# Attention weights of the second sample divided by their sums on two engines instead of one

## The chip, the cores and the metric

The kernel runs on one core of a Trainium2 chip. A core has TensorE (matrix products, called PE in the profile), VectorE (DVE), ScalarE (ACT), GpSimd (POOL) and SyncE (SP), which issues most transfers. The metric is the device time of one execution in microseconds.

## The reference, cut to what matters

The model is one inference step of a four-layer network on 128 context tokens (the first sample, s = 0) and 128 latent tokens (the second, s = 1). Layers 0 and 3 mix tokens by an mLSTM, layer 1 by windowed attention with a learned sink, layer 2 by neighbourhood attention; each layer ends in a convolutional FFN. The change touches the attention of layers 1 and 2 alone:

```python
def _attend(q, parts, sink):
    scale = q.shape[-1] ** -0.5
    logits = []
    for k_, v_, bias in parts:
        s = jnp.einsum('bkgqd,bksd->bkgqs', q, k_).astype(jnp.float32) * scale
        if bias is not None:
            s = s + bias
        logits.append(s)
    ...
    p = jax.nn.softmax(jnp.concatenate(logits, axis=-1), axis=-1)
    out, off = None, 0
    for k_, v_, _ in parts:
        n = k_.shape[2]
        o = jnp.einsum('bkgqs,bksd->bkgqd', p[..., off:off + n].astype(v_.dtype), v_)
        out = o if out is None else out + o
        off += n
    return out
```

A context token reads the 128 context keys; a latent token reads 128 latent keys and 128 keys of a cache, so its weights are twice as wide. Each of 16 heads has its own softmax, whose last step divides the exponentials by their sum.

## The kernel before, in words

Every engine has an instruction list written out by hand; semaphores join them. Weights stream from memory as 1 MB tiles through four buffers `raw`; ScalarE rounds each half tile to `spl_hi` (L488), VectorE takes the remainder `spl_lo` (L499, 128x1024 values, both inputs in SBUF, the on-chip memory), and TensorE multiplies both parts. A buffer is loaded again once its tile is split or used. Between other work TensorE runs `fill`, which multiplies tiles of another stream, the modulation weights (L755).

Attention works in eight units of four heads. Unit u belongs to head group u // 2 and to sample u % 2, so odd units are those of the second sample, with weights of 256 columns a head instead of 128. A unit passes through:

- `scores` on TensorE (L1027), into the banks SCORES, of which there is one pair: the next unit's scores wait for the exponentials of this one.
- `maxima` on VectorE: the largest score of each head (L2217, in layer 2 for odd units L2223 to L2227), and its negative `nm` (L2230 in layer 1, L2236 in layer 2), a 128x4 instruction. L2230 reads `mx` and `nsink`, L2236 reads `mx`, all in SBUF.
- `exps` on ScalarE (L1566): exponentials into `Ea[u % 2]`, and their sums.
- `reciprocals` on VectorE (L2248): `rsum`, one number a head, and in layer 1 before it L2244.
- the division, on GpSimd (L2525): `Ea` times `rsum`, in place, one instruction for the four heads, with the semaphore `pn_done` at its end.
- `weights` on TensorE (L1043): transposes of `Ea`, after `pn_done`; copied out by ScalarE and, for odd units, VectorE (L2252).
- `values` on TensorE (L1063), copied out by ScalarE as `O_hi`, with the remainder `O_lo` from VectorE in `attended` (L2257).

The units overlap: VectorE's list in layer 1 reads, from unit 3 on, `maxima(u)`, `reciprocals(u)`, `weights(u - 1)` when u - 1 is odd, `attended(u - 2)`, `maxima(u + 1)`. In layer 2 the projections of the queries, keys and values (`half_rows`, L692) lie between the units of the first half, and VectorE's list holds their splits (L499) and the copies of their results to `qrow`, `krow` and `vrow` (L2200). TensorE waits for such a copy (semaphore `row_d`) before it starts the projection that reuses the bank, at L1155 and L1165.

Of the kernel before, what the change touches and what calls it, by code (L numbers as in the profile page):

```python
# [19 lines left out]
ALU = mybir.AluOpType  # L20
# [3 lines left out]
P = 128  # L24
# [4 lines left out]
TOK = NS * T  # L29
# [284 lines left out]
def build(nc, io):  # L314
# [128 lines left out]
    def v3(ap, b):  # L443
        return ap.rearrange("p (a b) -> p a b", b=b)
# [4 lines left out]
    def beside(t, g, e):  # L449
# [13 lines left out]
        z_silu z_mul z_hi z_lo  # L463
        up_hi up_sum tg_done cg_half cg_done tv_done cv_half cv_done sg_done gt_done ghi_done glo_done
        cache_landed bias_landed row_a row_d row_k row_v roped tq_mm tq_a tq_d tk_mm tk_a tk_d kv_landed
        s_mm nm_done exp_done esink_in esink_done rsum_done pn_done pt_mm pt_a pt_d o_mm o_hi o_lo
        xa_done yt_mm yrow_a yrow_d y_landed""".split()
    S = {n: nc.alloc_semaphore(n) for n in names}
    raw_landed = [S[f"raw{r}"] for r in range(RAW)]
# [83 lines left out]
    with nc.Block() as block:  # L553
# [41 lines left out]
        def _(pe):  # L595
# [387 lines left out]
            def attention(i):  # L983
# [48 lines left out]
                def weights(u):  # L1032
                    s = u % 2
                    w = 8 * a + u
                    pe.wait_ge(S["pn_done"], w + 1)
                    if w:
                        pe.wait_ge(S["pt_a"], w)
                    if w // 2:
                        pe.wait_ge(S["pt_d"], w // 2)
                    for b in range(1 + s):  # L1040
                        for p in range(4):
                            o = (4 * b + p) * T
                            mm = pe.transpose(ACC[2 + b][:, p * T:(p + 1) * T], Ea[s][:, o:o + T], ident)  # L1043
                    mm.then_inc(S["pt_mm"], 1)
# [720 lines left out]
        def _(dve):  # L1765
# [424 lines left out]
            def attention(i):  # L2190
# [48 lines left out]
                def reciprocals(u):  # L2239
                    w = 8 * a + u  # L2240
                    dve.wait_ge(S["exp_done"], 4 * w + 4)
                    if a == 0:
                        dve.wait_ge(S["esink_done"], w + 1)
                        link(dve.tensor_tensor(sums[:, :], sums[:, :], esink[:, :], ALU.add))  # L2244
                        link.wait()
                    if w:
                        dve.wait_ge(S["pn_done"], w)
                    dve.reciprocal(rsum[:, :], sums[:, :]).then_inc(S["rsum_done"], 1)  # L2248

                def weights(u):  # L2250
                    dve.wait_ge(S["pt_mm"], 8 * a + u + 1)
# [204 lines left out]
        @block.gpsimd  # L2456
        def _(pool):
            chain = Link(pool, "pool_chain")
            zeroed = [gI, gF, gA, gM, gb, gc, gG, gz]
            for t in zeroed:  # L2460
                pool.memset(t[:, :], 0.0).then_inc(S["misc_init"], 1)
            pool.memset(half_pow[:, :], -0.5).then_inc(S["misc_init"], 1)
            assert len(zeroed) + 1 == MISC_INIT

            pool.memset(credit[0:1, 6:7], 0.0).then_inc(S["xcs_done"], 2)
            pool.wait_ge(S["misc_init"], MISC_INIT)
            pool.wait_ge(S["loads"], 16)

            def square_total(q):

                done = 3 * q
                for k in range(3):
                    pool.wait_ge(S["sq_done"], 5 * q + (2, 3, 3)[k])
                    if k:
                        pool.wait_ge(S["sqa_done"], done + k)
                    elif q:
                        pool.wait_ge(S["ssq_mm"], q)
                    out, a, b = ((sqa[:, :], sq[0][:, :], sq[1][:, :]), (sqa[:, :], sqa[:, :], sq[0][:, :]),
                                 (sqa[:, 0:TOK], sqa[:, 0:TOK], sqa[:, TOK:2 * TOK]))[k]
                    pool.tensor_tensor(out, a, b, ALU.add).then_inc(S["sqa_done"], 1)  # L2480

            def norm(q):
                square_total(q)
                pool.wait_ge(S["xvar_done"], q + 1)
                pool.tensor_tensor(rstd[:, :], var[:, :], half_pow[:, :], ALU.pow).then_inc(S["rstd_done"], 1)

            for i in range(DEPTH):
                norm(2 * i)
                if MIXER[i] == "mlstm":
                    j = ML_INDEX[i]  # L2490
                    for t in range(8):
                        pool.wait_ge(S["xc_done"], 8 * j + t + 1)
                        o = COL["ml_skip"] + j * KI + 2 * t
                        skip = small[:, o:o + 2]
                        pool.tensor_tensor(v3(XCS[:, t * 512:(t + 1) * 512], TOK), v3(ow[t % 2][:, :], TOK),
                                           skip.unsqueeze(2).to_broadcast([P, 2, TOK]),
                                           ALU.mult).then_inc(S["xcs_done"], 1)
                    for h in range(MH):
                        q = 4 * j + h
                        weights = v3(ST[:, h * TOK:(h + 1) * TOK], TOK)  # L2500
                        pool.wait_ge(S["e_done"], 5 * q + 5)
                        if h >= 2:
                            pool.wait_ge(S["den_mm"], q - 1)
                        pool.tensor_tensor(v3(Pw[h % 2][:, :], TOK), v3(E[h % 2][:, :], TOK),
                                           weights.to_broadcast([P, 2, TOK]), ALU.mult).then_inc(S["p_done"], 1)
                        pool.wait_ge(S["den_done"], q + 1)
                        pool.wait_ge(S["den_mm"], q + 1)
                        chain(pool.tensor_tensor(Pw[h % 2][:, :], Pw[h % 2][:, :], den[h % 2][:, :], ALU.mult))
                        chain.wait()
                        pool.tensor_tensor(PT[:, h * TOK:(h + 1) * TOK], Pw[h % 2][:, 0:TOK], Pw[h % 2][:, TOK:2 * TOK],  # L2510
                                           ALU.add).then_inc(S["pt_done"], 1)
                    for h in range(MH):
                        q = 4 * j + h
                        pool.wait_ge(S["var_done"], q + 1)
                        if q:
                            pool.wait_ge(S["hn_done"], 2 * q)
                        chain(pool.tensor_scalar(var[:, :], v3(mv[:, :], 2)[:, :, 1], 1.0, EPS, ALU.mult, ALU.add))
                        chain.wait()
                        pool.tensor_tensor(rstd[:, :], var[:, :], half_pow[:, :], ALU.pow).then_inc(S["root_done"], 1)
                else:  # L2520
                    for u in range(8):
                        width = (1 + u % 2) * T
                        pool.wait_ge(S["rsum_done"], 8 * (i - 1) + u + 1)
                        ev = v3(Ea[u % 2][:, 0:4 * width], width)
                        pool.tensor_tensor(ev, ev, rsum[:, :].unsqueeze(2).to_broadcast([P, 4, width]),  # L2525
                                           ALU.mult).then_inc(S["pn_done"], 1)
                norm(2 * i + 1)

            norm(2 * DEPTH)
# [22 lines left out]
```

## Time and profile before

| What | Value |
|---|---|
| Time, median of 3 runs | 1843.75 us (1842.93 to 1846.68) |
| The profiled execution's own time | 1840.74 us |
| Its span, first to last instruction | 1839.1 us |
| TensorE busy | 1793.7 us, 98% |
| VectorE busy | 1389.5 us, 76% |
| ScalarE busy | 1002.4 us, 55% |
| GpSimd busy | 143.8 us, 8% |
| HBM traffic | 228 GB/s over the span |
| The granted clock of TensorE, mean | 0.996 |

The attention units of layer 1 lie between 655 and 705 us of the span, those of layer 2 between 960 and 1041 us. A share of busy time is a mean over stages; in both stretches the other engines hand work to and fro in short steps, and who waits for whom is read from the timeline.

### The profile page before, as it was taken

The page shows a single profiled execution, that of the slowest core. Times are in us where ns is not written, and L with a number is a line of the kernel's source. Part 1 is how long each engine was busy: PE and PEld are TensorE (multiplying, and loading weights), DVE is VectorE, ACT ScalarE, POOL GpSimd, SP SyncE. Part 2 cuts the span into 40 slices and gives each one's busy share as a digit, 9 for nine tenths or more (in the row PEclk, how much of TensorE's full clock was granted, in tenths as well). Part 3 has the DMA queues.
Part 4 walks back from the last instruction along what each step waited for, and adds up shares of the span by engine and source line. Part 5 has one row for each costly group of instructions (what it writes and reads, how often), then busy time and mean ns, then how long its engine had stood idle before and what let it go on. Part 6 is the DMA issues. An engine that isn't in the chain of part 4 may idle for free.

```text
span 1839.1 us, 27506 instructions
## 1 busy us (share of the span) xinstructions
PE 1793.7 (98%) x11032; PEld 1494.3 (81%) x11032; DVE 1389.5 (76%) x2140; ACT 1002.4 (55%) x1567; POOL 143.8 (8%) x122
## 2 busy tenths in 40 slices
PE   5999999999999999999999999999999999999998
PEld 3988877797888867888977778888888787878888
DVE  3854777668898767999865698988665877779984
ACT  3744445446674454776354466745653445456753
POOL 1100121000000011000101100001100210010001
PEclk8999999999999999999999999999999999999999
DMA  9565656857665766675674777566555746445552
GB/s 393 211 225 197 203 207 242 307 221 292 261 216 205 288 250 265 252 277 198 216 311 166 298 283 294 204 224 266 207 185 183 240 163 225 171 172 195 197 173 80
DMA packets 74318, 421.27 MB, mean 229 GB/s; under 512 B 12400, under 2 KB 18952, under 8 KB 26576
## 3 DMA queue, kind: packets, MB, share of 16 engines
q1 hardware_dynamic: 56016, 395.68, 57.5%
q10 hardware_dynamic: 18176, 23.85, 4.0%
q8 instruction: 87, 1.43, 0.3%
q14 instruction: 39, 0.32, 0.0%
HBM read 408.51 MB, written 10.96 MB: 228 GB/s over the span
## 4 chain that ended last, share of the span: by engine, by line
PE 86%; DVE 5%; issue 3%; DMA 2%; ACT 2%; POOL 1%; SPq 0%; ACTq 0%; POOLq 0%; DVEq 0%
PE ps L654 17%; PE ps L676 10%; PE ps L711 9%; PE ps L657 9%; PE ps L636 6%; PE ps L692 5%; PE ps L714 5%; PE ps L639 3%; PE ps L622 3%; PE ps L624 3%; PE ps L623 3%; PE ps L755 3%; DMA raw<-in_stream 2%; DVE spl_lo L499 2%; PE ps L962 1%
## 5 line engine op out<-in xcount | busy, mean ns | idle before, releaser
L499 DVE TENSOR_TENSOR spl_lo<-raw,spl_hi 128x1024 fp32r<-128x1024 f32 x556 | 690.0, 1266 | 148.4 <-ACT spl_hi L488 147.1
L488 ACT ACTIVATE spl_hi<-raw 128x1024 fp32r<-128x1024 f32 x556 | 574.2, 1053 | 299.9 <-PE ps L714 109.5
L654 PE MATMUL ps<-H,spl_hi 128*128 128x512 f32 x1408 | 444.4, 397 | 3.7 <-DVE H L1854 2.9
L657 PEld LDWEIGHTS ps<-H,spl_lo 128*128 128x128 f32 x1408 | 264.5, 188 | 62.5
L657 PE MATMUL ps<-H,spl_lo 128*128 128x256 f32 x1408 | 276.7, 278 | 0.0
L654 PEld LDWEIGHTS ps<-H,spl_hi 128*128 128x128 f32 x1408 | 214.3, 189 | 17.9 <-issue 14.2
L711 PE MATMUL ps<-G,spl_hi 128*128 128x512 f32 x528 | 165.8, 395 | 0.0
L636 PE MATMUL ps<-B,spl_hi 128*128 128x512 f32 x512 | 160.8, 395 | 0.0
L622 PE MATMUL ps<-H,spl_hi 128*128 128x256 f32 x512 | 148.3, 290 | 1.8 <-DVE spl_lo L499 1.1
L623 PE MATMUL ps<-H,spl_hi 128*128 128x256 f32 x512 | 145.2, 284 | 0.0
L624 PE MATMUL ps<-H,spl_lo 128*128 128x256 f32 x512 | 145.0, 283 | 0.0
L676 PE MATMUL ps<-spl_hi,A 128*128 128x512 f32 x512 | 140.0, 391 | 0.5 <-ACT v L1267 0.5
L714 PEld LDWEIGHTS ps<-G,spl_lo 128*128 128x128 f32 x528 | 99.2, 188 | 23.4
L639 PEld LDWEIGHTS ps<-B,spl_lo 128*128 128x128 f32 x512 | 96.2, 188 | 22.7
L676 PEld LDWEIGHTS ps<-spl_hi,A 128*128 128x128 f32 x512 | 95.2, 188 | 21.7 <-issue 2.3
L755 PE MATMUL ps<-raw,cond_wide 128*32 128x512 f32 x704 | 94.6, 632 | 17.3 <-DMA raw<-in_stream 17.3
L1267 ACT ACTIVATE up<-ps 128x512 f32<-128x512 f32 x88 | 52.6, 598 | 105.2 <-PE ps L657 105.1
L622 PEld LDWEIGHTS ps<-H,spl_hi 128*128 128x128 f32 x512 | 98.4, 192 | 11.5 <-issue 9.8
L714 PE MATMUL ps<-G,spl_lo 128*128 128x256 f32 x528 | 103.7, 278 | 0.0
L639 PE MATMUL ps<-B,spl_lo 128*128 128x256 f32 x512 | 100.6, 278 | 0.0
L623 PEld LDWEIGHTS ps<-H,spl_hi 128*128 128x128 f32 x512 | 98.5, 192 | 0.8 <-issue 0.7
L624 PEld LDWEIGHTS ps<-H,spl_lo 128*128 128x128 f32 x512 | 98.5, 192 | 0.0
(251 smaller groups left out, 2927.4 us busy)
## 6 DMA issues: line engine op xcount, KB each, us to landing
raw<-in_stream SPq DMA_DIRECT2D x366, 1024.0 KB, 5.0
out_new_C<-c_stage ACTq DMA_DIRECT2D x16, 512.0 KB, 3.8
column<-in_ada_cols SPq DMA_DIRECT2D x16, 512.0 KB, 5.3
cond_all<-cond_out ACTq DMA_DIRECT2D x3, 1024.0 KB, 7.3
ada_b<-in_ada_b ACTq DMA_DIRECT2D x3, 768.0 KB, 9.1
E<-rows_out ACTq DMA_DIRECT2D x8, 256.0 KB, 4.3
Em<-rows_out ACTq DMA_DIRECT2D x8, 256.0 KB, 4.5
x<-in_x SPq DMA_DIRECT2D x1, 1024.0 KB, 6.7
```

The costliest lines, as they stand in the source:

```text
L488: act.activation(spl_hi[m % SPL][:, :], raw[r % RAW][:, h * HALF:(h + 1) * HALF], ACT.Copy).then_inc(S["hi_done"], 1)
L499: dve.tensor_tensor(spl_lo[m % SPL][:, :], raw[r % RAW][:, h * HALF:(h + 1) * HALF], spl_hi[m % SPL][:, :].bitcast(F32), ALU.subtract).the ...
L622: pe.matmul(out, w_hi, x_hi, start=st, stop=False, skip_group_check=True)
L623: pe.matmul(out, w_hi, x_lo, start=False, stop=False, skip_group_check=True)
L624: mm = pe.matmul(out, w_lo, x_hi, start=False, stop=en, skip_group_check=True)
L636: pe.matmul(v3(banks[b][:, :], TOK), spl_hi[m % SPL][:, c], B_both[:, kk], start=kk == 0, stop=False, skip_group_check=True)
L639: mm = pe.matmul(banks[b][:, 0:TOK], spl_lo[m % SPL][:, c], B_both[:, kk, 0], start=False, stop=kk == KI - 1, skip_group_check=True)
L654: pe.matmul(banks[:, b * 512:(b + 1) * 512], spl_hi[m % SPL][:, c], H[:, kk * 512:(kk + 1) * 512], start=kk == 0, stop=False, skip_group_c ...
L657: mm = pe.matmul(banks[:, b * 512:b * 512 + TOK], spl_lo[m % SPL][:, c], H[:, kk * 512:kk * 512 + TOK], start=False, stop=kk == KD - 1, sk ...
L676: mm = pe.matmul(ACC[2 * s + c][:, :], a, w[m % SPL][:, c * 512:(c + 1) * 512], start=st, stop=en, skip_group_check=True)
L711: pe.matmul(v3(bank[:, :], TOK) if nk == KI else bank[:, :], spl_hi[m % SPL][:, b], rows(k), start=st, stop=False, skip_group_check=True)
L714: mm = pe.matmul(ps[2 * pair + o][:, 0:TOK], spl_lo[m % SPL][:, b], x_hi, start=False, stop=en, skip_group_check=True)
```

## The change

In an odd unit GpSimd now divides the weights of the first two heads only (128x512 values instead of 128x1024). VectorE, right after its reciprocal, divides those of the other two, with two instructions of 128x256 values, and signals a new semaphore `pn_half`; TensorE's transposes of an odd unit wait for both semaphores. Even units stay as they are. VectorE first waits for its own reciprocal (`rsum_done`), which is also what GpSimd waits for.

```diff
--- before.py
+++ after.py
@@ -463,7 +463,7 @@
         z_silu z_mul z_hi z_lo
         up_hi up_sum tg_done cg_half cg_done tv_done cv_half cv_done sg_done gt_done ghi_done glo_done
         cache_landed bias_landed row_a row_d row_k row_v roped tq_mm tq_a tq_d tk_mm tk_a tk_d kv_landed
-        s_mm nm_done exp_done esink_in esink_done rsum_done pn_done pt_mm pt_a pt_d o_mm o_hi o_lo
+        s_mm nm_done exp_done esink_in esink_done rsum_done pn_done pn_half pt_mm pt_a pt_d o_mm o_hi o_lo
         xa_done yt_mm yrow_a yrow_d y_landed""".split()
     S = {n: nc.alloc_semaphore(n) for n in names}
     raw_landed = [S[f"raw{r}"] for r in range(RAW)]
@@ -1033,6 +1033,8 @@
                     s = u % 2
                     w = 8 * a + u
                     pe.wait_ge(S["pn_done"], w + 1)
+                    if s:
+                        pe.wait_ge(S["pn_half"], w // 2 + 1)
                     if w:
                         pe.wait_ge(S["pt_a"], w)
                     if w // 2:
@@ -2246,6 +2248,12 @@
                     if w:
                         dve.wait_ge(S["pn_done"], w)
                     dve.reciprocal(rsum[:, :], sums[:, :]).then_inc(S["rsum_done"], 1)
+                    if u % 2:
+                        dve.wait_ge(S["rsum_done"], 8 * a + u + 1)
+                        for k in range(2, 4):
+                            o = slice(k * TOK, (k + 1) * TOK)
+                            ins = dve.tensor_scalar(Ea[1][:, o], Ea[1][:, o], rsum[:, k:k + 1], None, ALU.mult)
+                        ins.then_inc(S["pn_half"], 1)
 
                 def weights(u):
                     dve.wait_ge(S["pt_mm"], 8 * a + u + 1)
@@ -2521,8 +2529,9 @@
                     for u in range(8):
                         width = (1 + u % 2) * T
                         pool.wait_ge(S["rsum_done"], 8 * (i - 1) + u + 1)
-                        ev = v3(Ea[u % 2][:, 0:4 * width], width)
-                        pool.tensor_tensor(ev, ev, rsum[:, :].unsqueeze(2).to_broadcast([P, 4, width]),
+                        n = 4 - 2 * (u % 2)
+                        ev = v3(Ea[u % 2][:, 0:n * width], width)
+                        pool.tensor_tensor(ev, ev, rsum[:, 0:n].unsqueeze(2).to_broadcast([P, n, width]),
                                            ALU.mult).then_inc(S["pn_done"], 1)
                 norm(2 * i + 1)
 
```

VectorE's list around the reciprocal of unit 3 in layer 1, before. `sums`, `rsum` and `mx` are the sums, their reciprocals and the maxima; `Ea_128` in the second list is the buffer of the odd units.

```order
L2244 TENSOR_TENSOR sums<-sums,esink 128x4 [waits esink_done,exp_done]
L2248 RECIPROCAL rsum<-sums 128x4 [waits pn_done,dve_link]
L2257 TENSOR_TENSOR O_lo<-ps,O_hi 128x2x128 [waits o_hi]
L2217 TENSOR_REDUCE mx<-ps 128x2 [waits s_mm]
L2217 TENSOR_REDUCE mx<-ps 128x2
L2230 SCALAR_TENSOR_TENSOR nm<-mx,nsink 128x4 [waits dve_link]
L2233 TENSOR_TENSOR esink<-nm,nsink 128x4 [waits nm_done]
```

The same place in the changed kernel:

```order
L2246 TENSOR_TENSOR sums<-sums,esink 128x4 [waits esink_done,exp_done]
L2250 RECIPROCAL rsum<-sums 128x4 [waits pn_done,dve_link]
L2255 TENSOR_SCALAR Ea_128<-Ea_128,rsum 128x256 [waits rsum_done]
L2255 TENSOR_SCALAR Ea_128<-Ea_128,rsum 128x256
L2265 TENSOR_TENSOR O_lo<-ps,O_hi 128x2x128 [waits o_hi]
L2219 TENSOR_REDUCE mx<-ps 128x2 [waits s_mm]
L2219 TENSOR_REDUCE mx<-ps 128x2
L2232 SCALAR_TENSOR_TENSOR nm<-mx,nsink 128x4 [waits dve_link]
L2235 TENSOR_TENSOR esink<-nm,nsink 128x4 [waits nm_done]
```

Two multiplications stand between the reciprocal and the `O_lo` of unit 1, ahead of the maxima of unit 4. The same two stand behind the reciprocal of every odd unit, eight times in all.

GpSimd's list at the start of layer 1's units, before:

```order
L2525 TENSOR_TENSOR Ea_127<-Ea_127,rsum 128x512 [waits rsum_done]
L2525 TENSOR_TENSOR Ea_128<-Ea_128,rsum 128x1024 [waits rsum_done]
L2525 TENSOR_TENSOR Ea_127<-Ea_127,rsum 128x512 [waits rsum_done]
L2525 TENSOR_TENSOR Ea_128<-Ea_128,rsum 128x1024 [waits rsum_done]
L2525 TENSOR_TENSOR Ea_127<-Ea_127,rsum 128x512 [waits rsum_done]
```

And in the changed kernel:

```order
L2534 TENSOR_TENSOR Ea_127<-Ea_127,rsum 128x512 [waits rsum_done]
L2534 TENSOR_TENSOR Ea_128<-Ea_128,rsum 128x512 [waits rsum_done]
L2534 TENSOR_TENSOR Ea_127<-Ea_127,rsum 128x512 [waits rsum_done]
L2534 TENSOR_TENSOR Ea_128<-Ea_128,rsum 128x512 [waits rsum_done]
L2534 TENSOR_TENSOR Ea_127<-Ea_127,rsum 128x512 [waits rsum_done]
```

The instructions of the odd units (`Ea_128`) have half as many columns; nothing else has moved there.

## Rows read from the trace of the kernel before

**Rows 1.** Page: the span, and the chain that ended last, by engine.

```profile
span 1839.1 us, 27506 instructions
...
PE 86%; DVE 5%; issue 3%; DMA 2%; ACT 2%; POOL 1%; SPq 0%; ACTq 0%; POOLq 0%; DVEq 0%
```

**Rows 2.** Groups, GpSimd: count | busy us, mean ns | idle before.

```profile
L2525 POOL TENSOR_TENSOR Ea<-Ea,rsum 128x1024 f32<-128x1024 f32 x8 | 15.1, 1893 | 40.7 <-DVE rsum L2248 40.7
...
L2525 POOL TENSOR_TENSOR Ea<-Ea,rsum 128x512 f32<-128x512 f32 x8 | 8.3, 1040 | 123.9 <-DVE rsum L2248 123.9
```

**Rows 3.** Waits of TensorE: us in total, times, longest us.

```profile
PE ps L1043 <- POOL Ea L2525: 4.5, 5, 2.0
```

**Rows 4.** The chain in order of time, layer 1: start us, us, what.

```profile
679.01 1.50 ACT Ea L1566 x8
...
683.22 0.17 DVE nm L2230
...
685.40 0.72 PE ps L1027 x8
...
689.63 1.07 PE ps L1027 x8
```

**Rows 5.** Timeline of VectorE, layer 1: start us, us; idle before it in brackets.

```profile
667.80 0.68 DVE L1773 TENSOR_TENSOR mod_b<-ps,ada_b 128x512 f32<-128x512 f32 x1
...
669.17 0.70 DVE L2230 SCALAR_TENSOR_TENSOR nm<-mx,nsink 128x4 f32<-128x4 f32 x1
...
685.74 0.18 DVE L2248 RECIPROCAL rsum<-sums 128x4 f32<-128x4 f32 x1
...
686.24 0.42 DVE L2257 TENSOR_TENSOR O_lo<-ps,O_hi 128x256 fp32r<-128x256 f32 x1 [0.31 <-ACT O_hi L1267]
...
687.36 0.56 DVE L2230 SCALAR_TENSOR_TENSOR nm<-mx,nsink 128x4 f32<-128x4 f32 x1
```

**Rows 6.** Timeline of GpSimd, layers 1 and 2 (odd units).

```profile
667.97 1.89 POOL L2525 TENSOR_TENSOR Ea<-Ea,rsum 128x1024 f32<-128x1024 f32 x1 [3.59 <-DVE rsum L2248]
...
686.00 1.89 POOL L2525 TENSOR_TENSOR Ea<-Ea,rsum 128x1024 f32<-128x1024 f32 x1 [3.80 <-DVE rsum L2248]
...
975.83 1.89 POOL L2525 TENSOR_TENSOR Ea<-Ea,rsum 128x1024 f32<-128x1024 f32 x1 [5.77 <-DVE rsum L2248]
...
992.77 1.90 POOL L2525 TENSOR_TENSOR Ea<-Ea,rsum 128x1024 f32<-128x1024 f32 x1 [8.50 <-DVE rsum L2248]
...
1023.73 1.89 POOL L2525 TENSOR_TENSOR Ea<-Ea,rsum 128x1024 f32<-128x1024 f32 x1 [6.01 <-DVE rsum L2248]
```

**Rows 7.** Timelines of VectorE and GpSimd in a norm, 713 to 717 us.

```profile
713.23 1.22 DVE L499 TENSOR_TENSOR spl_lo<-raw,spl_hi 128x1024 fp32r<-128x1024 f32 x1
...
713.38 2.21 POOL L2480 TENSOR_TENSOR sqa<-sq,sq 128x512 f32<-128x512 f32 x1 [16.55 <-ACT sq L1284]
...
714.36 2.32 DVE L499 TENSOR_TENSOR spl_lo<-raw,spl_hi 128x1024 fp32r<-128x1024 f32 x1
```

**Rows 8.** Timeline of VectorE, layer 2.

```profile
977.00 2.94 DVE L499 TENSOR_TENSOR spl_lo<-raw,spl_hi 128x1024 fp32r<-128x1024 f32 x2 [1.25 <-ACT spl_hi L488]
...
994.21 2.67 DVE L499 TENSOR_TENSOR spl_lo<-raw,spl_hi 128x1024 fp32r<-128x1024 f32 x2 [0.53 <-ACT spl_hi L488]
...
1025.06 0.58 DVE L2236 TENSOR_SCALAR nm<-mx 128x4 f32<-128x4 f32 x1
```

**Rows 9.** Timeline of TensorE, layer 2.

```profile
980.64 0.47 PE L692 MATMUL ps<-spl_hi,H 128*128 128x512 f32 x1 [1.18 <-issue]
...
997.59 0.47 PE L692 MATMUL ps<-spl_hi,H 128*128 128x512 f32 x1 [0.19 <-issue]
...
1027.29 1.14 PE L1027 MATMUL ps<-kT,qT 64*128 64x256 f32 x8
```

**Rows 10.** Groups by line and form, VectorE.

```profile
L1991 DVE TENSOR_SCALAR gM<-gF 36x256 f32<-36x256 f32 x2 | 0.6, 277 | 0.0
...
L2452 DVE TENSOR_SCALAR yrow<-ps,rstd 128x256 f32<-128x256 f32 x4 | 1.7, 478 | 0.8 <-POOL rstd L2485 0.8
```


## The prediction

> **What bounds the kernel now.** The profile's page comes first: TensorE is busy for nearly the whole span and 86% of the chain that ended last is its own [rows 1]. So a microsecond that TensorE waits in attention is a microsecond of the time, unless it would have waited later anyway. Next, the list of TensorE's waits: it waited for GpSimd's division 5 times, 4.5 us in all [rows 3]. That is all that a faster division can hand to TensorE directly. The groups by form give the price of a division: 1893 ns for an odd unit, 1040 ns for an even one [rows 2], so that half the columns save 0.85 us.
>
> The chain then tells the two layers apart. In layer 1 from 655 us to 685.40 it runs between VectorE and ScalarE: maxima, `nm`, exponentials (1.50 us for an even unit), sums, reciprocal, and on to the next maxima [rows 4]. From 685.40 on it is TensorE's. In layer 2 it is mostly TensorE's, with short waits in it [rows 9].
>
> Last, the timelines show something that the groups hide. `nm` of unit 5 took 0.17 us [rows 4]; `nm` of unit 6 took 0.56, and that of unit 2 took 0.70 [rows 5]. Both ended when GpSimd's division did, at 686.00 + 1.89 = 687.89 and 667.97 + 1.89 = 669.86 [rows 6]. So VectorE is held up while GpSimd works. It is the same in layer 2: a pair of splits took 2.94 and 2.67 us, and the 0.58 us `nm` of unit 6 ended at 1025.64, when the division begun at 1023.73 was over [rows 6, 8]. The norm shows the other direction. Splits began at 713.23, GpSimd's addition at 713.38, the second split at 714.36. The first split took its normal 1.22 us. The addition ended at 715.59, that is 1.14 us after the first split; the second split took 2.32 us and ended 1.09 us after the addition [rows 7]. The engines took turns, and the waiting GpSimd went ahead of VectorE's next instruction. The first split's end at 714.45 also shows that an instruction that isn't held starts 0.09 us before the end of the one ahead.
>
> **The change, part by part.** Let r be the end of an odd unit's reciprocal. GpSimd starts at r + 0.08 (685.92 against 686.00) and before was done at r + 1.97 [rows 5, 6].
>
> *Price of one multiplication on VectorE.* No row shows 128x256 from SBUF to SBUF with one number a partition. The nearest are 277 ns (36x256, SBUF to SBUF) and, above, 478 ns (128x256 out of PSUM, with such a number) [rows 10]. I take 0.30 us, since the first has the same memories and columns.
>
> *What the two engines do together.* Both wait for `rsum_done`. VectorE follows itself in some 0.04 us (an estimate: `nm` of unit 5 began at 683.22 and ended at 683.39, and the next step shown in the chain waits no longer than that on it), GpSimd in 0.08. By the turns of [rows 7]: first multiplication until r + 0.34; then GpSimd, whose addition kept 1.14 us after its grant where I take 0.90 for the shorter division (1.04 less the same start of about 0.14 that ran while it was held), until r + 1.24; then the second multiplication, 0.19 us more, until **r + 1.43**. TensorE's weights are ready 0.54 us sooner than before, but VectorE goes on 1.43 us later. What stands behind it is, in turn, `mod_b` and the maxima, `O_lo` and the maxima, a split, or the maxima alone.
>
> *Layer 1, unit 1.* r = 667.89. `mod_b` began at 667.80 [rows 5]; now at 669.32 - 0.09 = 669.23, 1.43 later. `nm` (begun at 669.17) is then free at 670.60 and no longer held, and done at 670.77; before it was done at 669.87. Chain +0.90.
> *Unit 5.* r = 685.92, VectorE free at 687.35. `O_lo` began at 686.24 after 0.31 us idle; now at 687.26, +1.02. `nm` would end at 687.36 + 1.02 + 0.17 = 688.55 against 687.92: +0.63. Unit 3 is built in the same way (its `nm` too took 0.56 us) and costs +0.63.
> The exponentials of unit 6 are thus 2.16 us late. TensorE needs them for its scores at 689.63; they ended at about 687.95 + 1.50 = 689.45, so 0.18 us are slack [rows 4]. **Layer 1: +2.0.** Unit 7 adds nothing: no maxima follow it and the transposes behind are long covered by the output projection.
>
> *Layer 2, unit 1.* r = 975.75. VectorE is free at 977.18, the splits begin at 977.09 instead of 977.00 but are not held: they end at 977.09 + 2.35 = 979.44 against 979.94. The copy `qrow` behind them is what TensorE waited for, 1.18 us before 980.64 [rows 8, 9]: **-0.5**.
> *Unit 3.* r = 992.69, free at 994.12; `O_lo` and then the splits, from about 994.38, end at 996.73 against 996.88: **-0.15**, out of the 0.19 us that TensorE waited at 997.59.
> *Unit 5.* r = 1023.65, free at 1025.08. The maxima of unit 6 took 0.79 us up to `nm` at 1025.06, so began at 1024.27; now at 1024.99. `nm` ends at 1025.95 against 1025.64, +0.3. TensorE's next scores, at 1027.29 [rows 9], came 0.15 us after the exponentials ended (1025.64 + 1.50): **+0.2**. Unit 7's splits wait for a tile from memory: nothing.
> Layer 2: -0.45.
>
> **The sum** is 2.0 - 0.45 = **+1.6 us**. The profiled execution took 1840.74 us and would take 1842.3. That execution lies 3.0 us below the median of the runs, to which I add the same 1.6: **1845.3 us**. VectorE's eight pairs, 8 x 0.6 = 5 us of work, would be nothing to an engine that is 76% busy; they cost only where they lie in the chain.
>
> **A rule against the trace.** Whether the multiplication holds GpSimd out at all, no row shows: [rows 7] are instructions with two inputs in SBUF, and the `nm` of [rows 8], with one input, was the one that was held. The Trainium skill ("SBUF — State Buffer", section "Who interferes with whom") states that VectorE's `tensor_scalar`, when input and output are in SBUF, may run in a mode that takes the ports shared with GpSimd, and that whichever starts first keeps them for the whole instruction. By that rule the turns above hold; were the multiplication to use VectorE's own ports alone, it would be the first rival. That page of the Trainium skill advises to let the engine off the critical path wait, and here it is VectorE, on the path, that does.
>
> **The rivals.**
> *No turns: VectorE does both, or they don't hinder each other.* VectorE is free at r + 0.55, GpSimd done at r + 1.45 at the latest. In layer 1 `nm` of units 2, 4 and 6 comes at 0.0, -0.24 and -0.24, of which TensorE can use 0.2. In layer 2 unit 1 gives -0.45, unit 3 -0.19, unit 5 -0.5 (`nm` not held after 1025.1, and TensorE's transposes as much earlier), unit 7 -0.1. In sum -1.4: 1842.3. For it: the second multiplication is queued 0.2 us after the first, before a late GpSimd may have asked; against: GpSimd's addition, asked for 0.15 us after the split's start, went first.
> *Slower: the turns, at high prices.* If a multiplication takes 0.48 us (the upper row), GpSimd keeps the ports for its full 1.04 us and the second multiplication costs 0.33 after it, VectorE is free at r + 1.89, 0.46 later. That adds to three units of layer 1 and four places of layer 2: 7 x 0.46 = +3.2, in all +4.8: 1848.6. It decides from 0.3 us more, r + 1.73, on. For it: [rows 7] show grants of full length for VectorE; against: short instructions there lose only what they wait for.
> *Faster by more than measurable: the waits go.* If TensorE's 4.5 us for GpSimd vanished with nothing in their place, -4: 1839.8. Against it: only odd units change, and the chain between VectorE and ScalarE is no shorter.
>
> **How the numbers follow.** A change below 0.2% (3.7 us) can't be told from none by this measurement. My forecast, +1.6 with turns: 60%. No turns, -1.4: 23%. Both are within 0.2%, less a few per cent for runs that lie apart by as much as the three above (1842.93 to 1846.68). Slower with high prices: 13%. Faster: 4%. So faster 0.05, same 0.80, slower 0.15. The range reaches from the second case, less 1.3 for the runs' own spread, to the edge of the third: 1841.0 to 1849.0; the likeliest alone would be 1843.5 to 1847.5.
>
> **What would show it.** In the trace after: the multiplications (L2255) as a short one of 0.3 us and one of about 1.2 that ends after GpSimd; GpSimd's odd divisions about 1.15 us long instead of 1.89; `nm` in layer 1 at 0.17 us throughout; the exponentials of unit 6 about 2 us later, counted from those of unit 0; TensorE's wait at the first projection behind unit 1 in layer 2 down from 1.18 to 0.7 us. I am wrong if both multiplications are short (first rival), or if GpSimd goes first, which costs as much as the turns. I would be wrong in size if a later wait, say for a tile of weights, swallows the 2 us of layer 1; between 705 and 960 us I found no wait of TensorE that large.

## The result, and the profile after

The changed kernel took **1849.56 us** (median of 7 runs, 1847.53 to 1852.26) against 1843.75 (1842.93 to 1846.68). The ratio is 1.0031, with an interval of 1.002 to 1.0043: slower by 5.8 us, beyond the 1849.0 at which the predicted range ends. The profiled execution took 1850.99 us.

Two later sets of runs put the same pair at 1.0015 (1.0006 to 1.0024, +3.1 us) and 1.0014 (1.0005 to 1.0024, +2.3 us). All three intervals lie above 1, so the sign is firm; the size lies between 2 and 6 us. In the later sets the kernel before had medians of 1844.9 to 1845.2 us, some 1.3 above the first set's, and the changed kernel 1848.06 and 1847.48, 1.5 and 2.1 below its first. Why the sets differ by so much is open.

The page of the changed kernel: its span, and the chain that ended last, by engine, as in [rows 1].

```profile
span 1849.0 us, 27529 instructions
...
PE 87%; DVE 5%; issue 3%; DMA 2%; ACT 2%; POOL 1%; SPq 0%; ACTq 0%; POOLq 0%; DVEq 0%
```

The span is 9.9 us longer and the chain's shares are the same to a point: it is still TensorE's. Not all of the 9.9 us are the change's: layer 1's first `nm` begins at 660.12 us where it began at 657.83, so 2.3 us lie ahead of anything that was changed.

The sum was made in attention, so layer 1 comes first. VectorE behind the reciprocal of unit 1 (start us, us, then engine, line, operation; idle time before it in brackets). Lines L2217, L2230, L2244 and L2248 of before are now L2219, L2232, L2246 and L2250; the multiplications are L2255.

```profile
670.00 0.18 DVE L2250 RECIPROCAL rsum<-sums 128x4 f32<-128x4 f32 x1
670.21 1.50 DVE L2255 TENSOR_SCALAR Ea<-Ea,rsum 128x256 f32<-128x256 f32 x2
671.63 0.68 DVE L1775 TENSOR_TENSOR mod_b<-ps,ada_b 128x512 f32<-128x512 f32 x1
672.23 0.74 DVE L2219 TENSOR_REDUCE mx<-ps 128x2 f32<-128x256 f32 x2
673.00 0.16 DVE L2232 SCALAR_TENSOR_TENSOR nm<-mx,nsink 128x4 f32<-128x4 f32 x1
```

The pair of multiplications takes 1.50 us. `nm` is back at 0.16 us, as forecast (0.70 in [rows 5]). The two multiplications apart, from two narrow windows, are one of 1.23 us:

```profile
670.21 1.23 DVE L2255 TENSOR_SCALAR Ea<-Ea,rsum 128x256 f32<-128x256 f32 x1
```

and one of 0.34:

```profile
671.37 0.34 DVE L2255 TENSOR_SCALAR Ea<-Ea,rsum 128x256 f32<-128x256 f32 x1
```

GpSimd at the same place:

```profile
670.26 1.04 POOL L2534 TENSOR_TENSOR Ea<-Ea,rsum 128x512 f32<-128x512 f32 x1 [3.59 <-DVE rsum L2250]
...
682.37 1.04 POOL L2534 TENSOR_TENSOR Ea<-Ea,rsum 128x512 f32<-128x512 f32 x1 [5.97 <-DVE rsum L2250]
```

GpSimd's division takes 1.04 us, no more than an even unit's [rows 2], though it begins 0.05 us behind VectorE's in the records. So the turn went to **GpSimd first**: the first multiplication was held until GpSimd's division was over at 671.30 and ended 0.14 us later; the second ran free, in 0.34 us. All eight pairs look like this: over the 16 multiplications the durations are 339 ns at least and 1233 at most. The Trainium skill ("SBUF — State Buffer", section "Who interferes with whom") says that `tensor_scalar` within SBUF can take the ports shared with GpSimd, and that whichever of the two issues first keeps them. The trace agrees that a multiplication is held; by the recorded starts, with VectorE 0.05 us ahead, the one that began second went first here, so for the order the measurement decides. No run shows which of the multiplication's reads or writes is held.

VectorE is free at r + 1.53 (r = 670.18), where the forecast had r + 1.43. Then TensorE:

```profile
669.57 0.72 PE L1027 MATMUL ps<-kT,qT 64*128 64x128 f32 x8 [0.99 <-ACT Ea L1568]
672.36 1.11 PE L771 MATMUL ps<-small,mod_b 128*128 128x128 f32 x4 [2.07 <-DVE mod_b L1775]
673.27 1.91 PE L1045 MATMUL ps<-small,Ea 128*128 128x128 f32 x8
675.11 1.12 PE L1065 MATMUL ps<-PTa,vrow 128*64 128x128 f32 x8
676.16 2.04 PE L1027 MATMUL ps<-kT,qT 64*128 64x256 f32 x8
678.13 1.09 PE L1002 MATMUL ps<-small,qrow 128*128 128x128 f32 x8
```

The same instructions in the kernel before:

```profile
667.28 0.72 PE L1027 MATMUL ps<-kT,qT 64*128 64x128 f32 x8 [0.98 <-ACT Ea L1566]
668.53 0.66 PE L771 MATMUL ps<-small,mod_b 128*128 128x128 f32 x4 [0.54 <-DVE mod_b L1773]
669.91 1.09 PE L1043 MATMUL ps<-small,Ea 128*128 128x128 f32 x8 [0.72 <-POOL Ea L2525]
670.93 0.66 PE L1063 MATMUL ps<-PTa,vrow 128*64 128x128 f32 x8
671.52 1.14 PE L1027 MATMUL ps<-kT,qT 64*128 64x256 f32 x8
```

Two things differ. First, L771 waited 0.54 us for `mod_b` before and now waits 2.07. This is a wait that the forecast never priced: it saw `mod_b` late in VectorE's list and asked only what that does to the maxima behind it. Second, from then until 678 every group of matmuls takes 1.7 to 1.8 times as long: 1.91 for 1.09 (eight transposes), 1.12 for 0.66, 2.04 for 1.14. The windows of that stretch say why (columns: busy us and count of TensorE, of its weight loads, of VectorE, ScalarE, GpSimd; then the granted clock, the DMA share, GB/s):

```profile
668.00:672.00 4.00, 1.30 (x16) 0.53 (x8) 3.90 (x10) 2.10 (x10) 1.04 (x1) 0.90 0.96 334
672.00:676.00 4.00, 3.64 (x20) 3.14 (x20) 2.36 (x10) 2.20 (x10) 0.64 (x1) 0.50 0.81 336
676.00:678.00 2.00, 2.00 (x12) 1.21 (x8) 0.50 (x2) 0.38 (x1) 0.40 (x1) 0.50 0.00 0
1070.00:1080.00 10.00, 10.00 (x59) 5.11 (x59) 7.00 (x22) 6.01 (x18) 0.70 (x1) 0.83 0.98 410
```

In the kernel before (1062 to 1072 is the same piece of work as 1070 to 1080 above):

```profile
668.00:672.00 4.00, 2.75 (x24) 2.16 (x26) 2.36 (x8) 2.09 (x11) 1.86 (x1) 1.00 1.02 422
672.00:676.00 4.00, 4.00 (x44) 2.55 (x40) 3.18 (x9) 2.38 (x9) 1.04 (x1) 1.00 0.05 18
1062.00:1072.00 10.00, 9.54 (x64) 5.24 (x64) 7.56 (x23) 6.49 (x18) 0.70 (x1) 1.00 0.95 398
```

From 672 to 678 us the granted clock is 0.50, the 1.2 GHz level instead of 2.4. A mean of 0.90 from 668 to 672 puts the fall 0.8 us before 672, when TensorE had waited 0.99 us for exponentials and was in the wait of 2.07; the low clock lasts 6.8 us. It falls for 3.4 us in each of the norms behind the two layers as well (a mean of 0.58 from 732 to 736 us, and the last window above); in this profile of the kernel before it was 1.00 there.

In layer 2 what the forecast read from VectorE's list came as it said: the splits behind unit 1 take 2.35 us for 2.94, and `nm` of unit 6 takes 0.17 for 0.58 [rows 8]:

```profile
984.30 2.35 DVE L499 TENSOR_TENSOR spl_lo<-raw,spl_hi 128x1024 fp32r<-128x1024 f32 x2
986.58 0.68 DVE L2202 COPY qrow<-ps 128x512 f32<-128x512 f32 x1
...
1032.52 0.17 DVE L2238 TENSOR_SCALAR nm<-mx 128x4 f32<-128x4 f32 x1
```

In the list of TensorE's waits (us in total, times, longest) GpSimd's division of [rows 3] is gone; what the division touches is now:

```profile
PE ps L1027 <- ACT Ea L1568: 4.8, 7, 1.0
PE ps L771 <- DVE mod_b L1775: 4.0, 3, 2.1
...
PE ps L1045 <- DVE Ea L2255: 1.6, 1, 1.6
```

The same list of the kernel before:

```profile
PE ps L771 <- DVE mod_b L1773: 2.5, 3, 1.2
PE ps L1027 <- ACT Ea L1566: 2.2, 4, 1.0
```

The 4.5 us for GpSimd came back as 2.6 more for exponentials, 1.5 more for `mod_b` and 1.6 for VectorE's own division (in the last unit of layer 2, where before GpSimd was waited for 2.0).

To compare many kernels, one measure serves below: the time from the start of the first `nm` of a layer to the start of the last `O_lo` of its units, what lies between, and what lies behind, read from the starts in each profile (us). "Half clock" is how long the granted clock was 0.50 in layer 1's units.

| Profile | Layer 1 | between | Layer 2 | behind | half clock |
|---|---|---|---|---|---|
| before, three profiles | 44.51, 44.53, 44.54 | 261.22, 261.28, 260.29 | 76.94, 77.14, 76.97 | 798.60, 799.43, 799.35 | 0, 0, 0 |
| changed, three profiles | 49.32, 49.37, 47.29 | 261.22, 261.24, 260.16 | 77.62, 76.76, 76.77 | 800.72, 800.15, 800.44 | 6.8, 6.8, 0 |

The second and third profile of each are the controls of the next section. The mean difference is +4.1 in layer 1, 0.0 in layer 2 (two of three profiles have -0.2, the first lost 0.7 more, most of it in the last unit, where ScalarE waited 0.99 us for a tile from memory), +1.3 behind: +5.4 us. What lies ahead of layer 1 scatters by more than 2 us in both kernels (its first `nm` begins at 657.83, 659.32 and 660.35 us before, at 660.12, 659.98 and 658.14 in the changed one).

### The profile page after: what moved, and what is told of

It is laid out like the page before. It is cut to its first block, busy times and chain, and to the rows that moved or that the text cites. A ratio compares the mean times of both kernels' runs of the same rounds, so it can differ in the third digit from the quotient of the medians.

```text
span 1849.0 us, 27529 instructions
## 1 busy us (share of the span) xinstructions
PE 1800.1 (97%) x11032; PEld 1499.0 (81%) x11032; DVE 1398.2 (76%) x2156; ACT 1002.4 (54%) x1567; POOL 137.1 (7%) x122
## 3 DMA queue, kind: packets, MB, share of 16 engines
q8 instruction: 87, 1.43, 0.3%
## 4 chain that ended last, share of the span: by engine, by line
PE 87%; DVE 5%; issue 3%; DMA 2%; ACT 2%; POOL 1%; SPq 0%; ACTq 0%; POOLq 0%; DVEq 0%
PE ps L654 18%; PE ps L676 9%; PE ps L711 9%; PE ps L657 9%; PE ps L636 6%; PE ps L692 5%; PE ps L714 5%; PE ps L639 3%; PE ps L755 3%; PE ps L622 3%; PE ps L624 3%; PE ps L623 3%; DMA raw<-in_stream 2%; DVE spl_lo L499 1%; PE ps L962 1%
```

## The experiments

My theory was that the added cost is VectorE held by GpSimd (the ports), which makes TensorE wait in layer 1 behind unit 1 and brings the clock down. The rivals: the multiplications are simply too much work for VectorE; or something between or behind the layers, and not the attention, takes the time.

**One unit alone, and all the others.** A table chooses which odd units are divided on both engines; the second kernel has `SPLIT = (3, 5, 7, 9, 11, 13, 15)`.

```diff
+SPLIT = (1,)
...
-                    if s:
-                        pe.wait_ge(S["pn_half"], w // 2 + 1)
+                    if w in SPLIT:
+                        pe.wait_ge(S["pn_half"], SPLIT.index(w) + 1)
...
-                    if u % 2:
+                    if w in SPLIT:
...
-                        n = 4 - 2 * (u % 2)
+                        n = 2 if 8 * (i - 1) + u in SPLIT else 4
```

> Only unit 1 of layer 1 is divided on two engines, the other seven odd units as in the kernel before. Theory A (VectorE is held until 1.5 us after its reciprocal, which lengthens the chain, and in this unit TensorE's 2.1 us wait for mod_b lets the granted clock fall to 1.2 GHz for some 6 us): +1.0 us of chain and +2.0 us of clock, +3 us over the kernel before, and a stretch at clock 0.5 after that unit. Theory B (the chain alone costs, the low clock is hidden behind it): +1 us. Theory C (the cost is spread over the span and not in these units): +0.7 us, an eighth of the whole.

> The seven other odd units are divided on two engines, unit 1 of layer 1 as before. Theory A: no stretch at the low clock, the whole change less 3 us: +2.5 to +3 us over the kernel before. Theory B: +4.8 us. Theory C: +5 us.

Unit 1 alone: 1.001 (1.0001 to 1.0019), layer 1 at 47.81 us with 6.8 us at half the clock. The others: 1.0001 (0.9993 to 1.001), layer 1 at 46.21 at full clock. Over before these are +3.30 and +1.70, together +5.0, where both at once gave +4.8: in layer 1 the parts add up. Of unit 1's 3.3, some 2.0 come with the half clock; at full clock its share is +1.0 (worked out in the next section), less than the +1.7 of the others. By the times the two kernels are slower than before by 1.8 and 0.4 us (medians 1846.81 and 1845.41 against 1845.02), where theory A had +3 and +2.5 to +3: both sizes were missed, and only their sum, +2.2, fits the two later sets of the changed kernel.

**`mod_b` ahead of the multiplications.** The same two multiplications, but TensorE's wait at L771 is taken away.

```diff
-                    reciprocals(1)
-                    copy_mod(i, 1)
+                    reciprocals(1, lambda: copy_mod(i, 1))
```

(`reciprocals` calls it between the reciprocal and the multiplications.)

> The changed kernel with the copy mod_b of layer 1 moved ahead of the two multiplications of unit 1, so that TensorE's transposes of it wait 1.5 us less; the maxima of unit 2 come as late as in the changed kernel. Theory A: TensorE's wait for mod_b is back near 0.5 us, the clock stays at full, 2 us less than the changed kernel: +3.5 to +4 us over the kernel before. Theory B: as the changed kernel, +5.8 us.

Layer 1 took 46.69 us at full clock; the wait at L771 was 0.53 again. The time was 1.0013 (1.0004 to 1.0022), +2.1 us, which is what layer 1's +2.2 says, and less than the +3.5 to +4 expected: without the long wait the chain between VectorE and ScalarE is still late. It is 0.6 us less late than in the changed kernel at full clock (47.29, below), because `mod_b` now runs while GpSimd holds the multiplications: the copy and the pair together take as long as the pair alone did, and `nm` comes 0.6 us sooner.

**TensorE kept busy in the gap.** Eight matmuls of no use stand ahead of L771.

```diff
+                    pe.wait_ge(S["row_a"], 2)
+                    pe.wait_ge(S["row_d"], 2)
+                    for _ in range(8):
+                        pe.matmul(ACC[0][:, :], H[:, 0:P], H[:, 0:512], start=True, stop=True, skip_group_check=True)
```

> The changed kernel with eight matmuls of 512 columns, whose result nothing reads, placed on TensorE between the scores of unit 2 and the transposes of mod_b in layer 1; they fill 1.7 of the 2.1 us that it waits there. Nothing comes earlier. Theory A: the clock stays at full, 2 us less than the changed kernel, +3.5 to +4 us over the kernel before. Theory B: as the changed kernel, +5.8 us.

Layer 1 took 47.28 us at full clock and the whole 1.0019 (1.001 to 1.0028), +3.0 us. At first I read this as proof that the idle time brings the clock down. It is not: the third profile of the changed kernel, without the added matmuls, has the same 47.29 at full clock with the wait of 2.07 in place:

```profile
670.38 0.66 PE L771 MATMUL ps<-small,mod_b 128*128 128x128 f32 x4 [2.07 <-DVE mod_b L1775]
670.87 1.04 PE L1045 MATMUL ps<-small,Ea 128*128 128x128 f32 x8
671.84 0.66 PE L1065 MATMUL ps<-PTa,vrow 128*64 128x128 f32 x8
672.78 1.14 PE L1027 MATMUL ps<-kT,qT 64*128 64x256 f32 x8 [0.28 <-ACT Ea L1568]
```

So the long wait is followed by the half clock in some executions and not in others, and neither the fill nor `mod_b` ahead shows anything on that. The same rows show that the wait of 2.07 us costs nothing by itself: layer 1 is as long with it as with the matmuls in its place.

**Controls.** The kernel before and the changed one, run again in two sets.

> The kernel before once more, beside the three others. All theories: no difference from itself; its ratio shows what this measurement tells from nothing. By stages of its trace, the span from the first nm of layer 1 to the last O_lo of its units took 44.5 us, and should again.

> The changed kernel once more, on the chip of the others. Its units of layer 1 took 49.3 us, 4.8 us more than before, those of layer 2 0.7 more. If the whole of the loss lies there, it is slower by 4 to 6 us again; with the low clock at the same place in the trace.

> The kernel before, a third profile: does the clock stay at full in layer 1's units? In two of its profiles it did, but it fell there in the kernel that changes layer 2 alone, whose layer 1 is the same code. If its steps stay 44.5 us at full clock here too, the low clock is rare without the change; if not, it is chance in every kernel and the share of the change in it is smaller than 2 us.

> The changed kernel, a third profile. If its 2.1 us wait for mod_b brings the low clock every time, layer 1 takes 49.3 us again; if it is chance, 47.3 us with the clock at full. Time: 3 to 6 us over the kernel before, as in the two measurements so far (5.8 and 3.1 us).

Before: 0.9999 (0.9991 to 1.0008) and 0.9994 (0.9985 to 1.0004). Changed: 1.0015 (1.0006 to 1.0024) and 1.0014 (1.0005 to 1.0024). Their stages are in the table above. What repeats to 0.1 us is layer 1 at a given clock; what scatters by about 1 us is the stretch between and the stretch behind, and by over 2 us the stretch ahead.

The mean granted clock of every run is known as well, and it limits what the table shows. The three profiles of the kernel before ran at 0.996, 0.997 and 0.997, while the 152 runs of that kernel in the four later sets have a mean of 0.9944 (0.989 to 0.998): the usual execution has more half clock than these three show. The changed kernel's 30 runs have a mean of 0.9938, none above 0.996. The difference of 0.0006 has the right sign, but the runs of one kernel scatter by 0.002, so it is hardly clear of chance.

**All four heads on VectorE in odd units, GpSimd out.** Twice the multiplications, but nothing beside them.

```diff
-                        for k in range(2, 4):
+                        for k in range(4):
...
-                        ins.then_inc(S["pn_half"], 1)
+                        ins.then_inc(S["pn_done"], 1)
...
+                        if u % 2:
+                            continue
```

> In odd units VectorE divides all four heads, GpSimd none. If the two engines hinder each other as the trace of the changed kernel shows (first multiplication 1.23 us, second 0.34), then twice the multiplications without GpSimd beside them are done sooner: four of 0.34 us, VectorE free 1.1 us after the reciprocal instead of 1.5. Layer 1: 1.2 us less than the changed kernel, and 2 us less again if TensorE's wait for mod_b, then 1.7 us, no longer lowers the clock. Rival, that each multiplication is slow by itself or that the work counts and not the ports: VectorE free after 2 us or more, slower than the changed kernel.

```profile
667.99 0.18 DVE L2248 RECIPROCAL rsum<-sums 128x4 f32<-128x4 f32 x1
668.20 1.14 DVE L2253 TENSOR_SCALAR Ea<-Ea,rsum 128x256 f32<-128x256 f32 x4
```

Four multiplications on their own take 1.14 us, less than two beside GpSimd (1.50); each takes 0.35. The kernel is at 0.9998 (0.9989 to 1.0006), layer 1 at 46.57 us with 3.4 us at half the clock, layer 2 at 75.93. Too much work for VectorE is thereby out as the main cause: doubling it makes the kernel no slower than before. It isn't free in layer 1: each of the pairs of steps around units 3 and 5, at full clock, takes 9.32 us, 0.38 more than before (0.7 to 1.1 more with GpSimd beside). Layer 2 gains 1.1.

**Two heads divided, by VectorE alone.** Heads 0 and 1 of odd units are left undivided, so this kernel leaves out a part of the softmax; GpSimd idles there.

```diff
-                        ins.then_inc(S["pn_half"], 1)
+                        ins.then_inc(S["pn_done"], 1)
...
+                        if u % 2:
+                            continue
```

> Work is left out: in odd units VectorE divides heads 2 and 3 and nobody divides heads 0 and 1, so GpSimd is idle there. The order of all else is that of the changed kernel. It prices the two multiplications without GpSimd beside them. If the ports are what costs: 0.6 us for the two instead of 1.50, TensorE's wait for mod_b 1.2 us instead of 2.1, and the units of layer 1 take 44.5 to 45.2 us instead of 49.3, as in the kernel before. If the instructions themselves cost: 47 us or more.

```profile
670.32 0.62 DVE L2253 TENSOR_SCALAR Ea<-Ea,rsum 128x256 f32<-128x256 f32 x2
670.85 0.69 DVE L1773 TENSOR_TENSOR mod_b<-ps,ada_b 128x512 f32<-128x512 f32 x1
```

0.62 us for the pair, layer 1 at 44.82 us, within 0.3 of before, at full clock; L771 waits 1.19 us; the time is 0.9995 (0.9986 to 1.0003). The same VectorE instructions with GpSimd beside them took 47.29 at full clock. **The 2.5 us between are what GpSimd's simultaneous work costs**, one profile against one, and the whole agrees: 0.9995 without it, 1.0014 and 1.0015 with it. GpSimd's own part isn't what is waited for, since it is over 0.4 us before VectorE's pair. That it costs through shared ports is the reading of the held and unheld durations.

**The multiplications behind the maxima.** In four units VectorE divides after the next `nm`, when GpSimd is done.

```diff
-                    if u % 2:
-                        dve.wait_ge(S["rsum_done"], 8 * a + u + 1)
...
+                def divided(u):
+                    dve.wait_ge(S["rsum_done"], 8 * a + u + 1)
...
+                    divided(1)
```

(`divided(u)` has the loop over the two heads. It stands behind `maxima(u + 1)` for units 1, 3 and 5 of layer 1 and unit 5 of layer 2; for the other four odd units it stands right behind the reciprocal, as in the changed kernel. The reciprocal also waits for `pn_half` of the unit before.)

> The division on two engines, but VectorE's two multiplications stand behind the next unit's maxima (units 1, 3, 5 of layer 1 and 5 of layer 2), where VectorE waits 1.5 us for ScalarE. My theory: GpSimd is done by then, nothing in the chain is late, nm is no longer held: layer 1 takes 43.7 to 44.5 us, layer 2 0.2 less than before; within 1 us of the kernel before or faster by 1. Rival, that a division which ends 0.2 us later than before holds TensorE back: layer 1 45 us or more.

```profile
670.17 0.66 PE L771 MATMUL ps<-small,mod_b 128*128 128x128 f32 x4 [0.54 <-DVE mod_b L1775]
671.80 1.76 PE L1045 MATMUL ps<-small,Ea 128*128 128x128 f32 x8 [0.97 <-issue]
673.49 1.12 PE L1065 MATMUL ps<-PTa,vrow 128*64 128x128 f32 x8
```

The pair took 0.61 us in the four moved places, still 1.50 in the other four, and the chain kept its 4.08 us a step in unit 1, but now TensorE's weights come late: the transposes began 0.97 us after L771 and the clock fell for 3.4 us. Layer 1 took 46.74 us where 43.7 to 44.5 was expected, the whole 1.0002 (0.9993 to 1.0011). The rival that was named came true: units 3 and 5, at full clock, cost 0.3 us each as well. The wait had moved from `mod_b` to the weights.

**Layer 2 alone.** The split there only, `SPLIT = (9, 11, 13, 15)`, run in two sets; and the odd units of layer 2 on VectorE alone, layer 1 as before.

> The division on two engines in layer 2 alone. Layer 1 as before (44.5 us); layer 2 0.2 to 0.4 us shorter than before, as in the trace of the second run of the changed kernel. If the low clock that the changed kernel's trace shows in the norm behind layer 2 belongs to this layer's units, it is here too and the stretch behind takes 1 us more; if it belongs to what layer 1 has shifted, it isn't. Time within 1.5 us of the kernel before.

> The division on two engines in layer 2 alone, again. Its trace showed 0.3 us less in layer 2 than before and nothing elsewhere, its times 3.5 us less by the medians (ratio 0.9988). If the times were right, it is faster by 2 us or more again; if the trace is, no difference can be told.

> Layer 1 as before; in layer 2 VectorE divides all four heads of odd units, GpSimd none. From the trace of the kernel in which VectorE does so in both layers: layer 1 44.5 us, layer 2 75.9 instead of 77.0, the rest as before: 1.1 us faster, less than this measurement can tell. Rival, that the gain of layer 2 is lost in the norm behind it: no difference in the span either.

The split: 0.9988 (0.9979 to 0.9996) at first, then 0.9999 (0.999 to 1.0008). The traces have layer 2 at 76.82 and 76.75 us against 77.0, so 0.2 to 0.3 us of gain; the 3.5 us of the first set have no place in the trace and did not come again. The two ratios of this one kernel lie 0.0011 apart, more than the half width of either interval, so a single set doesn't settle differences of 2 us. All on VectorE: layer 2 at 75.90 us, a gain of 1.1, and 0.9996 (0.9986 to 1.0006). In that last kernel layer 1 is the code of before, and yet:

```profile
672.00:676.00 4.00, 3.27 (x19) 2.48 (x20) 2.01 (x9) 2.59 (x11) 1.79 (x2) 0.65 0.88 371
```

```profile
671.45 0.66 PE L771 MATMUL ps<-small,mod_b 128*128 128x128 f32 x4 [0.53 <-DVE mod_b L1773]
672.83 1.65 PE L1043 MATMUL ps<-small,Ea 128*128 128x128 f32 x8 [0.72 <-POOL Ea L2534]
674.41 1.12 PE L1063 MATMUL ps<-PTa,vrow 128*64 128x128 f32 x8
```

The clock fell for 3.4 us behind waits of 0.99, 0.53 and 0.72, the waits of before, and layer 1 took 45.88, 1.35 more than at full clock. So a half clock here can come without the change. With unit 1 as before it came in one of seven profiles, for 3.4 us; with the wait of 2.07 us behind the one of 0.99, in three of four, for 6.8. That is more often and longer in these profiles, which are too few to show the rate.

**All on VectorE with `mod_b` ahead**, both of the above joined, as the best version the runs pointed to.

> VectorE divides all four heads of odd units in both layers, and the copy mod_b stands ahead of the multiplications of unit 1. The clock should stay at full in layer 1, which then takes 1 us less than with VectorE alone and mod_b behind: 45.4 us, still 0.9 more than before, since nm of the even units comes later; layer 2 75.9. In all 0 to 0.5 us faster than before, not to be told from none.

0.9996 (0.9988 to 1.0005), layer 1 at 46.09 us with 3.4 at half the clock, which did not stay at full as expected, layer 2 at 75.94. Not shown to beat before.

## Why the prediction was wrong

The turns on VectorE, the mechanism that the forecast rests on, came true. **Two steps failed.** The lateness that the turns cause in layer 1 was summed too small, +2.0 where the runs show +2.8 at full clock. And `mod_b`, late by 1.43 us, was followed in VectorE's list only, with TensorE's wait for it and TensorE's clock put at nothing; in the profiled execution the clock took 2.0 us more. Point by point:

- *Price of one multiplication*, 0.30 us: 0.34 to 0.35. Right.
- *What the two engines do together*, VectorE free at r + 1.43 by turns: r + 1.53, also by turns, but with GpSimd first. The prediction said that this order costs as much, and it does within 0.1 us. Of the signs it named, the 1.15 us division of GpSimd is wrong (1.04), the short and then long multiplication came as long and then short, and `nm` at 0.17 us is right.
- *Layer 1*, +2.0 us: **+2.8 at full clock**. Two steps from `nm` to `nm` around an odd unit, third profile of the changed kernel against before: unit 1 5.61 + 4.58 against 4.07 + 5.12, +1.00 (forecast +0.90); unit 3 5.26 + 4.77 against 4.13 + 4.80, +1.10 (+0.63); unit 5 5.26 + 4.42 against 4.14 + 4.80, +0.74 (+0.63); in all +2.8 where +2.16 was forecast. Unit 1's was well made. "Unit 3 is built in the same way" failed: 0.36 us come in unit 4's step, which is longer than unit 6's (4.77 against 4.42) for a reason I did not find: it lies between the start of ScalarE's `esink` and that of VectorE's sum, 0.67 us in unit 4 and 0.31 in unit 6, and it is there with GpSimd idle too. And the 0.18 us of slack that the forecast took off were not to be had, since TensorE's scores now wait for the exponentials after every odd unit (5 waits, 3.4 us, for 3 with 1.6).
- *Layer 2*, -0.45: -0.2 in two of three profiles. Its parts, by the same steps: unit 1 -0.39 (-0.5), unit 3 -0.07 (-0.15), units 5 and 6 together +0.35 (+0.2). The wait of 1.18 us ahead of the projection did not shrink to 0.7: TensorE's weights were ready sooner, so that it arrived sooner too, and waited 1.22.
- **The wait for `mod_b` and the clock, left out.** That TensorE waited 0.54 us for it already, and so would wait some 2 us right behind another of 1, was in the trace of before and was not read. The half clock behind it costs 49.3 - 47.3 = 2.0 us and came in two of three profiles of the changed kernel and in that of unit 1 alone. That the wait brings it down is not shown: the third profile has the wait at full clock, and the half clock came once behind the waits of before. The third profile also shows what is left without it: the forecast's +1.6 against +2.8 - 0.2 = +2.6 for both layers.
- **Behind the layers, left out.** In the norm behind layer 2 the clock was halved for 3.4 us in all three profiles of the changed kernel and in eight of eleven experiments (a ninth, the two heads alone, has it some 25 us sooner), never in three of before. The twelve profiles with it have 800.3 us behind layer 2 on the mean, the five without 799.1. That is +1.2 us, without a cause that I could show: the wait right ahead of it is the same in both kernels (0.84 us at L793), the split in layer 2 alone has it, so has the split in unit 1 of layer 1 alone, whose layer 2 is the code of before, and the two kernels with odd units on VectorE alone in both layers don't.

Together +2.8 + 1.4 (2.0 in two of three) - 0.2 + 1.2 = **+5.2 us**, which is what the profiles show (+5.4 by the table), and not what the runs do: 5.8, 3.1 and 2.3, a mean of 3.7. The profiles of before were executions at a high clock, so they put too much on the clock. Over all runs the clock differs by 0.0006, which is 1.1 us of an 1843 us span (an estimate from the mean clocks, as if TensorE were waited for throughout) instead of 1.4 + 1.2, and hardly clear of chance. Nor does the clock explain why the three sets differ: that of +5.8 has the highest mean clock of the changed kernel, 0.9949, against 0.9936 and 0.9933 in the others. What made the first set slower than the +2.6 of the layers by 3 us is open; in its profile 2.3 us lay ahead of layer 1. Of the rivals, "no turns" fell with the first profile; "slower with high prices" had the right sign and nearly the first size, 1848.6, for a wrong reason: its condition, VectorE free after r + 1.73, did not come true.

## What to carry to other kernels

Moving half of an operation to a second engine pays only if that engine isn't in the chain and isn't held by the first at that moment: here two multiplications of 0.34 us became 1.50 beside GpSimd, and four alone would have cost 1.14. When an instruction goes into an engine's list, follow everything queued behind it to whoever waits, also a small side product such as `mod_b`; a wait that grows next to another on TensorE may be followed by the half clock (three of four profiles here, not shown to be its cause), at 2.0 us in layer 1. Take several profiles of both kernels and compare the same stages in each before believing a difference of a few microseconds, and hold each profile's mean clock against that of all runs of its kernel before taking it for the usual one.

## What the runs showed of the hardware that was not expected

- Released by the same semaphore, GpSimd's division ran ahead of VectorE's first multiplication in all eight pairs, though VectorE's record begins 0.05 us earlier; the held multiplication took 1.23 us, the next 0.34.
- TensorE's granted clock fell to the 1.2 GHz level for 3.4 or 6.8 us at one place in some executions and not in others: behind waits of 0.99 and 2.07 us for 6.8 us in three profiles of four (two of them of one kernel, whose third stayed at full), behind 0.99, 0.53 and 0.72 for 3.4 us in one of seven. While it is down, groups of matmuls take 1.7 to 1.8 times as long (0.66 to 1.12, 1.09 to 1.91 us).
